# Nominal times of dense products whose first chunks are made one stage ahead

## The reference

```python
def hybrid_mixer(hn, w_in, ...):            # 528 tokens: 16 meta tokens and 512
    proj = hn @ w_in
    (dq, dk, dv, dz, da, db, sq, sk, sv, gate_dn, gate_sb) = jnp.split(proj, _split_points(), axis=-1)
    ...
    o_dn = gated_delta_rule(chunk_pad(q), chunk_pad(k), chunk_pad(v), chunk_pad(g), chunk_pad(beta))
    o_dn = rmsnorm(o_dn, dn_gain) * jax.nn.silu(heads(dz, DN_DV).astype(jnp.float32))
    qs = rmsnorm(heads(sq, SB_DH), sbq_gain)
    ks = rmsnorm(heads(sk, SB_DH), sbk_gain)
    o_sb = stick_breaking_attention(qs, ks, heads(sv, SB_DH)).astype(hn.dtype).reshape(B, T, SB_W)
    merged = jax.nn.sigmoid(gate_dn) * (o_dn @ w_branch_dn) + jax.nn.sigmoid(gate_sb) * (o_sb @ w_branch_sb)
    return merged @ w_out
```

## Time and profile before

| | us |
|---|---|
| median of three runs | 2264.19 (2261.4 to 2268.6) |
| the profiled execution | 2263.06 |
| its span, first to last instruction | 2261.3 |
| PE busy in the span | 2183.6 (97%) |
| the stages A to G together (with F) | 800.6, PE busy 770.4 |

### The profile page before, as it was taken

One profiled execution on the slowest core, in us unless ns is written; L12 is line 12 of the kernel. 1 busy time (PEld: TensorE's weight loads), 2 busy tenths in 40 slices (PEclk: granted clock), 3 DMA queues, 4 the chain that ended last, 5 costly groups with the idle time before them and its releaser, 6 DMA issues. The chain is left out here.

```text
span 2261.3 us, 32748 instructions
## 1 busy us (share of the span) xinstructions
PE 2183.6 (97%) x13572; PEld 1708.1 (76%) x13572; DVE 1109.2 (49%) x1771; ACT 803.3 (36%) x1315; POOL 101.7 (4%) x120
## 2 busy tenths in 40 slices
PE   8999799999999899989998999999999999999999
PEld 7776557888888899976765888767666678888887
DVE  3464675777733467654435534346432255444421
ACT  3432554444432453432214222225455433222211
POOL 0000133000000000000000000000012101000000
PEclk9999899999999999989999999999999999999999
DMA  4224001332222244322224331215721132232222
GB/s 163 75 65 149 10 1 66 95 98 96 94 93 93 76 158 146 113 91 71 63 65 151 132 100 58 71 57 174 240 73 56 39 107 86 96 98 94 93 93 93
DMA packets 76291, 214.46 MB, mean 95 GB/s; under 512 B 8432, under 2 KB 12912, under 8 KB 76144
## 3 DMA queue, kind: packets, MB, share of 16 engines
q1 hardware_dynamic: 76144, 212.37, 28.5%
HBM read 183.64 MB, written 27.66 MB: 93 GB/s over the span
## 5 line engine op out<-in xcount | busy, mean ns | idle before, releaser
L296 PE MATMUL ps<-nx_hi,whi 128*128 128x264 f32 (+1 forms) x1504 | 537.1, 357 | 16.9 <-DVE nx_lo L385 9.4
L274 ACT ACTIVATE whi<-raw 128x1024 fp32r<-128x1024 f32 x282 | 298.5, 1058 | 608.5 <-PE ps L298 438.7
L298 PE MATMUL ps<-nx_hi,wlo 128*128 128x264 f32 (+1 forms) x1504 | 512.3, 341 | 0.0
L281 DVE TENSOR_TENSOR wlo<-raw,whi 128x1024 fp32r<-128x1024 f32 x282 | 346.0, 1227 | 338.9 <-ACT whi L274 338.7
L297 PE MATMUL ps<-nx_lo,whi 128*128 128x264 f32 (+1 forms) x1504 | 512.2, 341 | 0.0
L296 PEld LDWEIGHTS ps<-nx_hi,whi 128*128 128x128 f32 x1504 | 286.7, 191 | 79.4 <-issue 44.4
L298 PEld LDWEIGHTS ps<-nx_hi,wlo 128*128 128x128 f32 x1504 | 286.9, 191 | 32.6
L297 PEld LDWEIGHTS ps<-nx_lo,whi 128*128 128x128 f32 x1504 | 287.4, 191 | 30.3 <-issue 1.9
L298 PE MATMUL ps<-x_hi,wlo 128*128 128x512 f32 x528 | 209.6, 397 | 0.0
L297 PE MATMUL ps<-x_lo,whi 128*128 128x512 f32 x528 | 208.3, 395 | 0.0
L296 PE MATMUL ps<-x_hi,whi 128*128 128x512 f32 x528 | 208.1, 394 | 0.0
(11 more groups left out here) (470 smaller groups left out, 2904.3 us busy)
## 6 DMA issues: line engine op xcount, KB each, us to landing
raw<-stream_dram SPq DMA_DIRECT2D x285, 512.0 KB, 3.5
qk_spill<-ring SPq DMA_DIRECT2D x16, 264.0 KB, 2.2
qk_cols<-qk_spill SPq DMA_DIRECT2D x16, 264.0 KB, 5.6
v_spill<-ring SPq DMA_DIRECT2D x16, 264.0 KB, 2.1
v_cols<-v_spill SPq DMA_DIRECT2D x16, 264.0 KB, 4.6
dz_spill<-ring SPq DMA_DIRECT2D x16, 256.0 KB, 2.1
dz<-dz_spill SPq DMA_DIRECT2D x16, 256.0 KB, 5.3
sbk_spill<-ring SPq DMA_DIRECT2D x8, 264.0 KB, 2.2
```

The costliest lines, as they stand in the source:

```text
L274: act.activation(K.whi[:, n % HL], K.raw[:, n % RAW], ACT.Copy).then_inc(K.s_hi, 1)
L281: dve.tensor_tensor(K.wlo[:, n % HL], K.raw[:, n % RAW], K.whi[:, n % HL].bitcast(F32), ALU.subtract).then_inc(K.s_lo, 1)
L296: pe.matmul(out, whi, xhi, start=start, stop=False, skip_group_check=skip)
L298: return pe.matmul(out, wlo, xhi, start=False, stop=stop, skip_group_check=skip)
```

## The change

`Products` gets an `at` of its own in place of that of `Lane`:

```diff
@@ -741,6 +741,12 @@
         self.parts = [len(operand(c)[2]) for c in range(n)]
         self.base = [0] + [int(x) for x in np.cumsum(self.parts)]
         K.at += n
+
+    def at(self, u):
+        led = self.led / self.n
+        if led >= 1:
+            return self.t0 + (self.t1 - self.t0) * u
+        return self.t0 + (self.t1 - self.t0) * (u - led) / (1 - led)
 
     def bank(self, c, h):
         return self.banks[(self.base[c] + h) % len(self.banks)]
```

## The result

The changed kernel takes 2274.5 us, the median of 4 runs (2272.2 to 2277.7), against 2263.3 for the kernel before: ratio 1.0055, 95% interval 1.0040 to 1.0071. It is slower by about 11 us.

The account below looks back on a forecast made before the run. PE was taken as the bound, with time to gain only where it idles or runs at the lower clock. A -1, B -4.7, C 0, D +1.7, E +2.5, G +2.5 sum to +1.0: forecast 2265, range 2257 to 2273.

Parts of the forecast that it names:

- the term of the clock: Start of stage D: PE's gap may again cost half of 3.41 us of work at the lower clock.
- G, +2.5 forecast: Stage G: seven thinned L1934 wait about 0.35 us each, +2.4; the 1.65 us start gain is not had; ends 0, +4.
- The thinning: Sums with one triple fewer ahead expose PE to waits: about +2 us in A, +1 in D, +2.4 in G.
- DVE's later evacuations push its own steps: Stage A: a few tenths of a us added to -1.7, giving -1.
- D, +1.7 forecast: Stage D: L1427 5.5 us later, PE idle about 2.75 us, clock may fall, thinning about +1; ends -0.5, +3.5.
- A, -1 forecast: Stage A: L1427 7.3 us late, 14 triples done early, net -2.2, clock -1.5, thinning about +2; ends -5, +2.
- B, -4.7 forecast: Stage B: idle ahead of L1196 falls from 7.8 to 4 us (-3.9), clock loss -0.8; ends -7, -2.
- My upper end: Stage B at -2 us: v_rows, their products behind a third split, come 2 us later and L1790 waits.
- E, +2.5 forecast: Stage E: the 3.30 us wait at L1790 grows to about 5.7 us; ends 0 and +4.5.
- The second: Rival: thinner fillers expose the chain in A, D and G, 0.3 us more at some 30 places, +9: 2274; chance 0.14.
- The third (the late raw chunk): Rival: late loads rule the starts; B's gap stays, D +2.5, E +4, together +8: 2272; chance 0.12.
- The first rival: Fillers keep PE busy at stage starts and the clock up: A -9, B -7, D and E 0, G -1: 2247; chance 0.18.

Follow-up runs that it names:

- Experiment 5: Kernel before with PE's triples spread in B, E, G; ACT, DVE, SP as before except the led chunk's evacuation; A with splits late; C, D unchanged: 2251.9 us.
- experiment 4: The change applied to the kernel before in stages D and G alone: 2274.1 us, ratio 1.0042.
- Experiment 6: The change in stage D alone against the kernel before, with nine useless half triples filling PE's wait ahead of L1427: 2263.5 us, ratio 1.0000.
- experiment 3: The change applied to the kernel before in stages A and B alone: 2263.0 us, ratio 0.9994.
- experiment 1: The change with led chunks' splits, stores and the loads behind those stores at old times; evacuations stay at the head: 2267.9 us, ratio 1.0021 to the kernel before.
- experiment 7: The whole change, plus each stage's first raw chunk loaded at the end of the stage in front: 2263.4 us, ratio 0.9998 to the kernel before.
- 10: The kernel before with only the early loads of each stage's first raw chunk: 2257.4 us, ratio 0.9978.
- 8: Kernel before with A's led splits late, B's loads and splits at the head with PE as before, other stages unchanged: 2255.5 us, ratio 0.9967.

## Why the prediction was wrong

The forecast was 2265, no change. It is 2274.5, slower by 0.55%. Two steps failed. The sum left later chunks' splits and evacuations where they were in G, and in the changed kernel they delay a softplus twice. And in D the term of the clock was mis-sized, with 3.41 us at the lower level for what became 10.24. In B a gain was counted that was given back, again in the later half.

**G, +2.5 forecast, +5.6 measured.** The steps are matched with those of the kernel before. The start is as worked out: the gain of 1.65 us is not had, and PE's delay stands at 5.1 us behind the first five sums, for seven triples (4.9 us) more ahead of them. The thinning is not. I had 0.35 us for each of seven sums. At five of them the delay falls by the full 0.70 us of the triple that is gone, so they cost nothing. At the other two it rises, from 5.1 to 5.8 and from 5.8 to 9.1 us, though a triple fewer stands there too: 5.5 us for the two. The waits of 1.14 and 2.12 us are 3.3 of it, and half of the 3.41 us at the lower clock is 1.7. What I left out was the other half of the change. I moved in my sum only what belongs to led chunks on ACT and DVE, and took the splits and evacuations of later chunks to stay where they were. They move too, in G by up to 0.9 of a chunk's old spacing. "DVE's later evacuations push its own steps" stands in my text at a few tenths, for A alone. Experiment 5 has the same order of PE and leaves these splits where they were: the delay peaks at 3.2 us and is down to -0.1 at the end. There a thinned sum costs 0.23 us on the average.

**D, +1.7 forecast, +4.7 and +5.5 measured.** The delay was right: L1427 5.5 us late by forecast, 5.7 measured; PE's wait 2.75 by forecast, 3.06 measured. The mis-sized term is the clock. I wrote that a gap of this size may take the lower level "again", at the 3.4 us of before. It took it for 10.24 us (13.65 in experiment 4), some 3 us of time. Experiment 6 shows that it is this. The thinning, +1 in my sum, cost nothing: from L1463 to its end D takes 176.6 us in every profile with the change's order of PE, and 181.7 to 181.8 in the others. These 5.1 us are what 13 half triples fewer (4.8 us) are worth. Part of the +4.7 comes from the profile of before, which had a short start of D by luck: an unchanged D has +1.1 to +2.7.

**A, -1 forecast, -2.1 and -1.9 measured.** Within what a profile tells: unchanged, A came out at -0.3 to -1.4. L1427 was to start 7.3 us late and starts 7.7 late. The 14 triples done early pay for it, as worked out, and the thinning takes about 1 us of that, not 2: behind L1463, A takes 171.2 us, and 180.2 in experiment 4, for 9.8 us less work. My reading of A's gaps was wrong in one point: of the 5.6 us idle in the first 12.4, only about 1.3 lie before the lower level begins at 1000.52.

**B, -4.7 forecast, -1.8 measured (-1.2 in experiment 3; unchanged, -1.0 and -1.1 in 6 and 4).** The first wait was to be 4.0 us and is 3.12, and the lower clock that the earlier trace rows shows there is gone, so that the early gain was larger than I had it. PE was 4 us ahead at 36 us and no longer at 49 us, through waits for DVE that hadn't been priced. With the splits left where they were, in experiment 5, these waits are gone and B keeps 4.5 us. My upper end named such a giving back, by another path (v_rows behind a third split).

**E, +2.5 forecast, +1.2 measured; C 0 forecast, +1.0 measured.** E in the range, though the one wait of 5.7 us at L1790 came as three, of 1.6, 2.9 and 0.6. C's +1.0 can't be told from nothing: it is +0.9 in experiment 3 too, where C is unchanged and has no wait for a bank (0.6 us in the changed kernel).

**The rivals.** The second gave 2274 and the time came out there, but not by its mechanism: experiment 1 has the same thin fillers and takes 8.1 us off A, experiment 5 has them in G at no loss, and behind L1463 D loses nothing by them. The third (the late raw chunk) was closer. With the chunk early, experiment 7 takes back all 11 us. Of that D is 6.9 us, where I had put the price in B and E. It isn't the whole cause, though, as G keeps +3.9 and experiment 5 repairs G without it. The rule of the Trainium skill that stood against the change (page "DMA: Bandwidth & Descriptors", section "Rules for kernel authors": issue early, wait late) is borne out by experiments 7 and 10: 11.1 us off the changed kernel, and 6.0 off the one before. The first rival's idea, that the fillers do what they are for, is true as well. It needed the splits out of the chain's way: 11.4 us in experiment 5.

The chances put 0.56 on no change. The cause is in the sum: in B and G each part was worked out at the start of the stage, where the change is easy to see, and little was asked of the middle. In D it was the start itself, and one execution stood for all.

## What to carry to other kernels

A change of nominal times moves every instruction that is ordered by them. List the crossings on each engine, of the later ones too, and price those that put something which waits (for a transfer, or for another engine's queue) ahead of a step that the critical engine needs. Work that fills gaps can be moved on the critical engine alone, and what feeds it can stay where it was. Here experiment 5 did this in B, E and G, moved the led chunks' splits back in A, and left C and D alone, which together turned +11 us into -11. A transfer that something at the head of a stage needs is issued at the end of the stage in front.

## What the runs showed of the hardware

Behind a wait of PE of 3.06 us in D, after a start in which it had worked, the granted clock was 0.50 for 10.24 us. With the wait filled by useless matmuls it was 1.00 in all of D. The level behind a gap isn't the same in every execution: D's start, with PE's order of before and the same wait of 1.40 us at L1427, came to L1463 1.0, 1.2, 1.2 and 2.7 us later in experiments 3, 10, 8 and 5 than in the profile of before, with the lower level there for 6.83 us or more in place of 3.41. So the one profile of before undersized what D's start cost in all four others.

The same 512 KB load took 3.9 us to its use where it was alone. It took 5.75 us in A of the changed kernel, issued at 1001.81 behind another load and a store and used at 1007.56, and 7.8 us in B of experiment 1 (1200.27 to 1208.04), among the loads of dz and qk_cols.
